# One split instruction for two neighbouring slabs of a weight ring, on ScalarE and on VectorE

## What is computed

```python
h = rmsnorm(x)
proj = h @ w_in              # z, xBC, dt, q, f, i, g, gate_a, gate_b
y = ssd(conv(xBC), dt) ...   # Mamba-2 branch: causal convolution, SiLU, chunked scan, 64 heads
o = hgrn2(q, f, i) ...       # HGRN2 branch, 16 heads
mixed = sigmoid(gate_a) * (y @ w_br_a) + sigmoid(gate_b) * (o @ w_br_b)
x = x + rmsnorm(mixed @ w_out)
x = x + rmsnorm(relu(rmsnorm(x) @ w_up) ** 2 @ w_down)       # hidden size 8192
x = x + sigmoid(rmsnorm(x) @ w_ple_gate) * (p @ w_ple_proj)
```

## Time and profile before

| | us |
|---|---|
| median of 3 runs | 2816.43 (2815.96 to 2818.28) |
| the profiled execution | 2817.92 |
| its span, first to last instruction | 2816.0 |
| TensorE busy | 2742.1 (97%) |
| VectorE busy | 1789.6 (64%) |
| ScalarE busy | 1425.6 (51%) |
| mean granted TensorE clock | 0.991 of full speed |

### The profile page before, as it was taken

The page is one execution under the profiler, slowest core; times in us unless marked ns, Lnnn a source line. Parts: engine busy times, 40 slices in busy tenths (PEclk is TensorE's granted clock), DMA queues, the critical chain, the costliest instruction groups (busy, mean ns, idle before and its releaser), DMA issues.

```text
span 2816.0 us, 59589 instructions
## 1 busy us (share of the span) xinstructions
PE 2742.1 (97%) x22075; PEld 2662.8 (95%) x22075; DVE 1789.6 (64%) x3208; ACT 1425.6 (51%) x2280; POOL 183.1 (7%) x297
## 2 busy tenths in 40 slices
PE   6999999999999999999979999989999999999999
PEld 5999999999999999999969999989999999999989
DVE  6878788744478887888854444566553345554475
ACT  5666666543356556556633333454443344443363
POOL 0111111100011111111110000000000000000000
PEclk9999999999999999999979999999999999999999
DMA  4544454455556665656535555535555545554534
GB/s 159 181 159 158 160 172 161 156 168 174 177 199 196 197 204 200 210 191 209 189 135 171 173 172 181 190 128 169 165 165 164 165 163 164 164 168 161 171 129 159
DMA packets 135286, 484.17 MB, mean 172 GB/s; under 512 B 17248, under 2 KB 19696, under 8 KB 134080
## 3 DMA queue, kind: packets, MB, share of 16 engines
q1 hardware_dynamic: 114560, 410.88, 43.8%
q0 software_dynamic: 20672, 72.55, 8.0%
HBM read 449.58 MB, written 33.78 MB: 172 GB/s over the span
## 4 chain that ended last, share of the span: by engine, by line
PE 88%; DVE 7%; ACT 2%; issue 1%; DMA 1%; POOL 0%; DVEq 0%; ACTq 0%; POOLq 0%
PE acc L1583 27%; PE acc L1585 26%; PE acc L1584 26%; DVE w_lo L967 1%; PE bank L1800 1%; PE bank L1846 1%; ACT w_hi L496 1%; PE bank L1749 1%; DVE ccv L1240 1%; PE bank L1830 1%; PE bank L1684 1%; PE bank L1766 0%; DVE x L1427 0%; DVE yf L1297 0%; DVE ht L1226 0%
## 5 line engine op out<-in xcount | busy, mean ns | idle before, releaser
L967 DVE TENSOR_TENSOR w_lo<-raw,w_hi 128x1024 fp32r<-128x1024 f32 x772 | 940.2, 1223 | 617.9 <-ACT w_hi L496 611.1
L1583 PE MATMUL acc<-h_hi,w_hi 128*128 128x288 f32 x3904 | 1169.6, 300 | 14.0 <-DVE h_lo L1003 11.5
L1584 PE MATMUL acc<-h_lo,w_hi 128*128 128x288 f32 x3904 | 1154.6, 296 | 0.0
L1585 PE MATMUL acc<-h_hi,w_lo 128*128 128x288 f32 x3904 | 1151.2, 295 | 0.0
L496 ACT ACTIVATE w_hi<-raw 128x1024 fp32r<-128x1024 f32 x772 | 811.3, 1055 | 463.8 <-PE acc L1585 408.0
L1583 PEld LDWEIGHTS acc<-h_hi,w_hi 128*128 128x128 f32 x3904 | 734.6, 188 | 21.7 <-issue 12.3
L1584 PEld LDWEIGHTS acc<-h_lo,w_hi 128*128 128x128 f32 x3904 | 735.9, 189 | 2.9
L1585 PEld LDWEIGHTS acc<-h_hi,w_lo 128*128 128x128 f32 x3904 | 737.7, 189 | 0.0
L1585 PE MATMUL acc<-u_hi,w_lo 128*128 128x288 f32 x1024 | 303.6, 296 | 0.0
L1583 PE MATMUL acc<-u_hi,w_hi 128*128 128x288 f32 x1024 | 302.6, 296 | 0.0
L1584 PE MATMUL acc<-u_lo,w_hi 128*128 128x288 f32 x1024 | 298.5, 292 | 0.0
(11 more groups left out here) (389 smaller groups left out, 3336.1 us busy)
## 6 DMA issues: line engine op xcount, KB each, us to landing
raw<-in_w SPq DMA_DIRECT2D x772, 512.0 KB, 3.3
ht<-in_ht POOLq DMA_DIRECT2D x64, 256.0 KB, 4.1
out_ssm_s<-ht POOLq DMA_DIRECT2D x64, 256.0 KB, 3.8
cbc<-cum_d POOLq DMA_DIRECT2D x8, 1152.0 KB, 6.9
hs<-in_s POOLq DMA_DIRECT2D x16, 512.0 KB, 4.5
out_hg_s<-hsn POOLq DMA_DIRECT2D x16, 512.0 KB, 5.0
x_in<-in_x SPq DMA_DIRECT2D x4, 576.0 KB, 6.0
mixb<-bmb POOLq DMA_DIRECT2D x16, 144.0 KB, 2.0
```

The source lines that it names most:

```text
L967: V.tensor_tensor(w_lo[:, k], raw[:, k], w_hi[:, k].bitcast(F32), ALU.subtract).then_inc(lo_done, 1)
L1583: M.matmul(out, w_hi[:, k, i], hi[:, kt0 + i], start=first and i == 0, stop=False)
L1584: M.matmul(out, w_hi[:, k, i], lo[:, kt0 + i], start=False, stop=False)
L1585: op = M.matmul(out, w_lo[:, k, i], hi[:, kt0 + i], start=False, stop=last and i == SK - 1)
```

## The change

Slots 0 and 1, and slots 2 and 3, are split by one instruction of 2048 columns on each of the two engines. The instruction stands where the split of the odd slot stood. The step of the even slot becomes empty. On ScalarE it waits for both loads and for the use of the slab that had the odd slot before (so also of the even one); it adds 2 to hi_done, and VectorE's adds 2 to lo_done. The first four slabs (m == 0) are split one by one as before. Loads stay one slab each: the two loads into a pair of slots are issued as soon as lo_done lets them, which is now at the same time. TensorE's waits are unchanged.

```diff
--- before.py
+++ after.py
@@ -489,11 +489,15 @@
     def _(act):
         def split_hi(m, k):
 
-            act.wait_ge(raw_in[k], (m + 1) * 16)
-            if not (isinstance(m, int) and m == 0):
-
+            if isinstance(m, int) and m == 0 or k % 2 == 1:
+                act.wait_ge(raw_in[k], (m + 1) * 16)
+            if isinstance(m, int) and m == 0:
+                nc.scalar.activation(w_hi[:, k], raw[:, k], ACT.Copy).then_inc(hi_done, 1)
+            elif k % 2 == 1:
+
+                act.wait_ge(raw_in[k - 1], (m + 1) * 16)
                 act.wait_ge(slab_used, m * RING + (k + 1 - RING))
-            nc.scalar.activation(w_hi[:, k], raw[:, k], ACT.Copy).then_inc(hi_done, 1)
+                nc.scalar.activation(w_hi[:, k - 1:k + 1], raw[:, k - 1:k + 1], ACT.Copy).then_inc(hi_done, 2)
 
         def ahead(first, per, it, s):
             split_hi(*slab(first, per, it, s + AHEAD))
@@ -963,8 +967,14 @@
 
         def split_lo(m, k):
 
-            dve.wait_ge(hi_done, m * RING + (k + 1))
-            V.tensor_tensor(w_lo[:, k], raw[:, k], w_hi[:, k].bitcast(F32), ALU.subtract).then_inc(lo_done, 1)
+            if isinstance(m, int) and m == 0:
+                dve.wait_ge(hi_done, k + 1)
+                V.tensor_tensor(w_lo[:, k], raw[:, k], w_hi[:, k].bitcast(F32), ALU.subtract).then_inc(lo_done, 1)
+            elif k % 2 == 1:
+
+                dve.wait_ge(hi_done, m * RING + (k + 1))
+                V.tensor_tensor(w_lo[:, k - 1:k + 1], raw[:, k - 1:k + 1], w_hi[:, k - 1:k + 1].bitcast(F32),
+                                ALU.subtract).then_inc(lo_done, 2)
 
         def ahead(first, per, it, s):
             split_lo(*slab(first, per, it, s + AHEAD))
```

## The result

The changed kernel took 2994.44 us (2993.59 to 2996.16), the kernel before 2816.43 us: a ratio of 1.063, 95% interval 1.061 to 1.065. The forecast was 2981. In the profiled executions the spans are 2993.2 and 2816.0 us, 177 us apart.

What follows compares the result with a forecast made beforehand. TensorE, 97% busy, was taken as the bound. HGRN 52.9, its clock 22, SSD 39.6 + 5.6 + 9.4, entries 30.6 and loops 5 sum to 165 us, on 2816.4 giving 2981 us; its own range 2940 to 3025, 70%.

Steps and rivals of the forecast that it cites:

- What bounds the kernel: Whole kernel: TensorE is busy 97% of the span; the splits are hidden, so time saved on ScalarE or VectorE is worth nothing.
- R3: Rival, whole kernel: faster, as TensorE's waits end on ScalarE and VectorE chains; at most -12 us, 2804; 2%.
- Lead: Every pair: the even slab is split two slabs ahead of TensorE instead of three, and is ready 1.94 us later.
- Price of a pair: ScalarE and VectorE: 1.94 + 0.03 + 2.28 = 4.25 us from a pair's start to ready, bounds 4.15 and 4.5.
- HGRN loop: From slab 0's start S, the next slab 0 starts at S+36.0 against S+32.4: +3.6 us in 14 iterations, 50.4.
- The clock: After HGRN stalls TensorE's clock is lower: 14 times 1.6, 22 us; 5.6 added in SSD, 3 behind the last two entries.
- R2: Rival: the clock stays low for two slabs after each HGRN stall, falls twice per SSD iteration: +39, 3020 us; 9%.
- R1: Rival: stalls in HGRN and entries, but the clock stays up and SSD absorbs most: +94, 2910 us; 17%.
- First HGRN iterations: HGRN loop's start: the first iteration, where the dt work leads, gets +2.5 us.
- SSD loop: Convolution chain between VectorE and ScalarE runs late: 7 times 5.65, 39.6 us, plus 5.6 for the clock.
- Entries: Starts of the other stages, where both slabs of a pair are now late: together 30.6 us, bounds 20 and 37.
- Loops with little else to do: Up and branch_a loops: pair ready about when the even slab starts, nothing or 0.1 us per pair; +5, bounds 0 and 15.

Runs made afterwards that it cites:

- e2: Changed kernel with each pair split by two 1024-column instructions per engine, counted by 2 only when the second is done; 3008.65 us, ratio 1.068.
- e3: Kernel before, with 72 of the 384 pairs merged, in the loops of branch_b, out and down; 2817.69 us, ratio 1.000.
- e8: Changed kernel with ScalarE's pair kept merged, VectorE splitting the two slabs one by one and counting each; 2938.82 us, ratio 1.043.
- e4: Changed kernel with 32 extra matmuls of 224 columns ahead of slab 0 in HGRN iterations 1 to 15; 2974.53 us, ratio 1.056.
- e1: Changed kernel with each pair split by two 1024-column instructions at the pair's place, each counted when done; 2863.08 us, ratio 1.017.
- e5: Changed kernel with HGRN's step 6, the next slab 0's pair, moved ahead of hso's wait (ScalarE) and hsg, hon, hso (VectorE); 2944.48 us, ratio 1.046.
- e7: Changed kernel with yt copied before the pair of step 8 on ScalarE in the SSD stage, instead of behind it; 2997.93 us, ratio 1.065.

## Why the prediction was right, point by point

- **What bounds the kernel.** Right: TensorE at 97%, split engines with time to spare. 26 and 33 us taken off VectorE and ScalarE gave 14 us on the path (e2), and 14 us off each gave nothing where there was slack (e3). The reading of the earlier trace rows was incomplete: with the second row for w_lo TensorE waited 8.4 us in 6, not 5.9 in 3, and R3 could have gained 15 us, not 12.
- **Lead.** Right, and the main cause: with two singles at the late place 47 us are lost, with one count for two slabs as well 192. The forecast said that an even slab is ready 1.94 us later; e8, where VectorE frees the even slab one split earlier, gives back 56 us.
- **Price of a pair.** 1.911 + 0.11 + 2.292 = 4.3 us between 253.75 and 258.06 in the timelines, forecast 4.25. The slopes from 1888 and 1536 columns held. Merging saves 0.07 us of VectorE's busy time per pair and 0.08 of ScalarE's (e2), within the forecast's "at most" of 0.2 and 0.1; the estimate of 60 us for VectorE compares with 26.
- **HGRN loop.** The cycle was worked out as S+16.7 (scan), S+31.5 (end of hso), S+36.0. In the iteration that begins at 220.26 the scan starts at 238.44, hso ends at 253.45 and slab 0 starts at 258.11; less some 1.5 for the clock at its head these are S+16.7, S+31.7 and S+36.3. The loop lost 74.2 against 72.8, and that close a match is partly luck: iterations 2 to 14 grew by 4.0 us each without the clock (e4), not 3.6, and the last of the 14 by only 0.2.
- **The clock.** Right in size in the HGRN loop, 22 us: the filler of e4 gives 22.5 back over 14 iterations. R2's longer fall was seen in two of them, those from 105.93 and 371.05 us, which took 38.6 and 39.1. R1 (clock stays up) is excluded for a gap of 3.7 us. The rival's evidence, an idle stretch without half clock behind it, was real: e1 and e5 show it for 1.2 and 1.3 us. Over the whole kernel, by the mean granted clocks of 0.991 and 0.972, the time at half clock rose from about 50 to about 165 us, which can have cost at most some 58 us; the forecast's three terms for the clock were 30.6, and only the HGRN part was measured by itself.
- **First HGRN iterations.** Mis-sized: 8.1 against 2.5. TensorE idles 2.6 us at 59 us in the kernel after, where it has no gap before, and the half clock behind that was not in the sum; the second iteration's 3.1 was not either.
- **SSD loop.** 38.5 against 45.2 with its clock. The chain was worked out well: the six convolutions come 1.4, 2.5, 3.5, 4.2, 4.2 and 5.2 us later, forecast 1.4, 2.5, 3.6, 4.4, 4.5 and 5.6, and six of the seven iterations take 86.55 us instead of 81.08. Where TensorE pays for it is partly another matter. In the two iterations from slab 232 and 252, TensorE's step from slab 8 to slab 9 grew by 2.5 and 3.3 us (forecast 2.4, yt). The next grew by 1.5 and 2.2, at half clock:

```profile
1156.50:1162.50 6.00, 6.00 (x28) 6.00 (x28) 5.86 (x13) 1.44 (x5) 0.60 (x2) 0.52 0.61 227
```

  The forecast had 0.8 of that per iteration. In exchange ysq gave back 0.7 instead of taking another 1.0, since slab 9 to 11 had already been delayed by more, and slab 14 added 1.0 in one iteration and nothing in the other. The iteration from slab 312, 1378.1 to 1464.7 us, has no half clock at all:

```profile
1378.10:1464.70 86.60, 82.59 (x610) 75.38 (x606) 66.12 (x115) 46.94 (x92) 13.29 (x24) 1.00 0.54 189
```

  It takes 86.55 us like the others. So the 5.6 us added for the clock were worth nothing here: a time lost to the clock counts as slack for what is late behind it, and the sum counted both. e7 shows the same from the other side.
- **Entries.** GB 3.3 for 5.5, branch_a 4.1 for 3.7, out 2.2 for 1.7, first up 10.1 for 8.0, second down 2.4 for 2.2, PLE 9.9 for 9.5, SSD's first iteration 10.8 for 9.4. All are of the right kind; no experiment took one apart.
- **Loops with little else to do.** The term with the largest relative miss: 13.1 us (4.5 + 3.7 + 4.9) against 5, inside its bounds of 0 and 15. The forecast put a pair's readiness and the even slab's start within 0.01 us of each other and took "nothing, or 0.1". Timelines of ScalarE and VectorE in the second up of the kernel after:

```profile
2494.78 1.92 ACT L500 ACTIVATE w_hi<-raw 128x2048 fp32r<-128x2048 f32 x1
...
2501.07 1.90 ACT L500 ACTIVATE w_hi<-raw 128x2048 fp32r<-128x2048 f32 x1
```

```profile
2496.80 2.29 DVE L976 TENSOR_TENSOR w_lo<-raw,w_hi 128x2048 fp32r<-128x2048 f32 x1 [1.47 <-ACT w_hi L500]
...
2503.08 2.29 DVE L976 TENSOR_TENSOR w_lo<-raw,w_hi 128x2048 fp32r<-128x2048 f32 x1 [1.30 <-ACT w_hi L500]
```

  From 2494.78 to the end of VectorE's half it is 4.31 us, from 2501.07 4.30: the hand-over costs 0.1 us, not the 0.03 of the sum. TensorE's steps between slabs there grow by up to 0.2 us, 0.3 per four slabs, and e8, which frees the even slab 1.1 us earlier, gives all of it back.
- **Loads.** Right: they land 0.6 us later and no wait of ScalarE for a slab is put down to them.

By the spans the loss is 12 us over the forecast's 165: +8 in the little-work loops, +6 in the first iterations, +5 in the other entries and the HGRN loop, −7 in SSD's loop.

What stays open: which part of each entry is the pair's lateness and which the clock; why e5 lengthened GB's entry; and whether a version exists that gains. Nothing tried was faster than the kernel before. Merging in slack and moving step 6 equal it, and with TensorE at 97% the waits that a shorter split could remove are the 8.4 us for w_lo and the 6.3 at L1800, 15 us at most.

## What to carry to other kernels

Merging two producer instructions of a ring takes lead from the first of the two: it is ready only when both are, and at the later one's place. Look for the waits on other work that stand between the two old places (hso here): they decide the price, not the duration saved. Time saved on an engine that is not the bound is worth nothing by itself, and a stall of the bounding engine of a few microseconds has a second price, the clock behind it, which in turn hides part of the next lateness.

## What the runs showed of the hardware

- An idle time of 3.7 us of TensorE was followed by half clock in every HGRN iteration, at about 1.5 us each. One of 2.6 us was followed by it in 8 of 14 iterations (e8), with the same gap each time. Ahead of slab 6 of iteration 0 the same 2.6 us were followed by it in the kernel after and not in e4. Idle times of 1.2 and 1.3 us in every iteration (e1, e5) left the clock at 1.00. More work, 32 small matmuls in the gap, made the changed kernel 20 us faster.
- An idle time ahead of slab 0 lengthened the iteration by 0.25 us more than its own length, at full clock: against 32.37 us before, gaps of 1.22 us in e1, 1.31 in e5 and 2.57 in e8 went with iterations of 33.85, 33.93 and 35.21 us. What the 0.25 us are is not shown.
- A split of 2048 columns takes 1.91 us on ScalarE and 2.29 on VectorE. Two back to back of 1024 take 2.36 on VectorE by their span (e8), so that merging saves 0.07 us there in a row, and 0.15 by the sum of the two durations, of which a part overlaps.
